# Five groups of context projections between the experts: one weight piece per block of products, two blocks per group at places of their own

## The chip, the cores and the metric

The kernel runs on one NeuronCore of a Trainium2 chip. It is one launch; everything is float32. The metric is the device time of one execution in microseconds; the median of three runs of the kernel before is 2745.36 us.

## The reference, cut to what matters

Two blocks of a model on a sequence of 256 tokens with 1024 features. The first block is a token mixer and then a feed-forward layer of 16 experts, each taking 34 of the 272 tokens. The second block is a bidirectional mixer of two branches (a gated delta rule, "gdn", and RWKV-7) that first runs over a context of 256 tokens to get its start states, and then over the tokens. The context's part does not depend on the first block, so the kernel computes it between the experts of the first block.

```python
# first block, per expert e (x16): xs are the 34 tokens that the router chose
hid = silu(xs @ w_gate[e]) * (xs @ w_up[e])      # w_gate, w_up: (1024, 2816)
y   = hid @ w_down[e] * g                        # w_down: (2816, 1024)
# second block, context: u_ctx is (256, 1024), w_in is (1024, columns)
a_ctx, b_ctx, _ = split(u_ctx @ w_in)
# gdn: k and v of the context: columns 512..1023 and 1024..1535, conv over time, silu, l2norm of k
# rwkv: k, v and the low-rank columns: 2064+512, 2064+1024 (512 each), 2064+1536 (256)
```

These five column groups are called k, v, rk, rv (512 columns each) and lo (256 columns). What is computed is the same before and after.

## The kernel before, in words

**The ring of weights.** All large weights pass through a ring of six slots in SBUF (`RING = 6`, a slot of `PIECE = 2816` floats in each of 128 partitions). `piece()` (in front of L170) numbers the pieces in the order in which the program will use them. SyncE (SP) issues them in that order at L871: piece n waits until the semaphore `piece_used` says that TensorE has released piece n-6. `piece_used` is one counter, so pieces are released in order too. An expert's gate and up weights come as 16 pieces (two for each 128 of the 1024 input features), its down weights as 8, each of 1408 KB with rows of 11 KB. `column_pieces(w, c0, cols)` makes two pieces of a column group of w_in, one for each half of the 1024 input features: for 512 columns 1024 KB each, with rows of 2 KB; for the 256 columns of lo 512 KB each, with rows of 1 KB.

**The experts' loop.** For each expert e (16) and each step k (8), TensorE runs `gate_up_pe(e, k)` (L3085): twelve products, in six pairs for six PSUM banks, matmuls at L3097, which need the two pieces of this step and release them at the last pair. After it come transposes of the hidden rows of expert e-1 (k = 0, 1; L3107), gathers of the chosen tokens for later experts (L2749, in expert 0 from k = 4 and in experts 1 and 2 in the middle of k = 1, 2), additions of finished experts (L3127) and the down products of expert e-1 (`down_pe`, L3120, k = 2 to 7). Expert e's hidden rows are made at its end: ScalarE's Silu of six banks (`silu_act`, L1119), VectorE's six products (L2048). The next expert's first matmul into a bank waits for that bank's product.

**Half steps.** The context's work is a Python generator on each of TensorE, ScalarE and VectorE. Each engine moves its generator on twice per step: in the middle of `gate_up_pe` (after the third of the six banks) and at the end of the step (not after k = 7). `slot_number(e, k)` is the number of the half step at the end of step (e, k); `until(n)` yields until half step n. The three engines count the same half steps, and all context work uses one PSUM bank, `bank_a`. What an engine does in one half step is queued in its program ahead of its share of the expert's next work, so a wait in a half step holds up the experts too.

**A column group before.** `AT_K = (0, 3)`, `AT_V = (2, 6)`, `AT_RK = (7, 1)`, `AT_RV = (8, 0)`, `AT_LO = (8, 4)`. Its two pieces stand in the ring's order behind the pieces of that step. TensorE's `project(name, cts)` (L2794) waits for both, computes two of four 128-column tiles (16 matmuls at L2802, listed as 32 by the profile), signals ScalarE, yields one half step, waits for ScalarE's copy out of `bank_a` (`landed_act`, L1136, copies at L1144), and computes the other two tiles; the first piece is released after 12 of those 16 matmuls, the second after 16. lo has two tiles only, so one block.

**What follows k.** VectorE convolves over time, one 128-row part per half step (L1800, L1802), ScalarE applies Silu (L1169), VectorE squares two parts (L1813), TensorE sums over features (L2854), ScalarE takes the root (L1175), VectorE the reciprocal and the product (L1815, L1816), and so for the other two parts one half step later. TensorE's first sum stands four half steps after the second block of products, in the middle of step (0, 6). Then TensorE turns k (L2814) at the ends of (1, 0) and (1, 1), and computes the gates at (1, 2). The group v goes through the conv and the Silu the same way, rk and rv through a time shift (L1911 to L1914) on VectorE.

## Time and profile before

| | |
|---|---|
| median of 3 runs | 2745.36 us (2738.47 to 2745.64) |
| the profiled execution | 2749.25 us, its span 2747.5 us |
| TensorE (PE) busy | 2425.6 us, 88% of the span |
| VectorE (DVE) busy | 893.0 us, 33% |
| ScalarE (ACT) busy | 447.5 us, 16% |
| GpSimd (POOL) busy | 85.5 us, 3% |
| moved by DMA | 789.10 MB, mean 287 GB/s |
| mean granted TensorE clock | 0.943 |

The profile's page gives busy times for each engine, the span in 40 equal slices of 68.7 us with the busy tenths of each engine in each slice, the DMA queues, the groups of instructions by source line with what ended their waits, and the DMA issues with their time to landing. A matmul's end is modelled, so a busy TensorE is not always TensorE at its peak. Busy shares are means over stages with different limits: the experts' loop lies in slices 6 to 26, the second block behind it. Answers to queries of the trace give the same for a stretch, an engine or a line.

### The profile page before, as it was taken

Reading aid. Unit: us, or ns where it says so; the run is one execution under the profiler, and the core shown is the slowest. Engines: PE = TensorE matmul, PEld = TensorE weight load, DVE = VectorE, ACT = ScalarE, POOL = GpSimd, SP = SyncE. Lnnn points to the kernel's source line nnn. Section 1 sums busy time; section 2 is a strip of 40 time slices with the busy share of each in tenths; the row PEclk is TensorE's granted clock in tenths of the full one; section 3 lists DMA queues with packets and bytes.
Section 4 is the critical chain, followed back from the end, with each engine's and each line's share of the span. In section 5 each row is a group of like instructions: output and inputs, shape, how many; then the busy total and the mean of one; then the engine's idle time right before and its main releaser. Section 6 shows DMA issues by size and latency. Waiting matters only on the chain. (4 is left out here: it accounts for less than half of the span.)

```text
span 2747.5 us, 42972 instructions
## 1 busy us (share of the span) xinstructions
PE 2425.6 (88%) x19453; PEld 1312.8 (48%) x19453; DVE 893.0 (33%) x1682; ACT 447.5 (16%) x810; POOL 85.5 (3%) x93
## 2 busy tenths in 40 slices
PE   7999799889999989999999999896595889599995
PEld 4544353333433434344444443275575877355552
DVE  3225534104222222313132221265556431332222
ACT  3112101101111101212121211231132220000001
POOL 0001000000000000000000000000001100000000
PEclk9998879999999999999999999998897999799998
DMA  5356348999999999999999999930010033479996
GB/s 191 116 180 225 143 173 324 400 418 377 411 422 423 408 378 380 421 412 403 415 408 421 413 400 408 393 109 16 2 39 2 4 128 123 167 290 422 422 423 279
DMA packets 129442, 789.10 MB, mean 287 GB/s; under 512 B 17493, under 2 KB 19805, under 8 KB 65133
## 3 DMA queue, kind: packets, MB, share of 16 engines
q1 hardware_dynamic: 125805, 773.78, 69.7%
q0 software_dynamic: 3456, 12.58, 1.2%
q8 instruction: 153, 2.51, 0.4%
q14 instruction: 28, 0.23, 0.0%
HBM read 774.79 MB, written 11.53 MB: 286 GB/s over the span
## 5 line engine op out<-in xcount | busy, mean ns | idle before, releaser
L3097 PE MATMUL bank<-ring,arena 128*34 128x462 f32 (+1 forms) x3072 | 680.3, 579 | 78.1 <-DMA ring<-in_w_up 57.5
L3097 PEld LDWEIGHTS bank<-ring,arena 128*34 128x34 f32 x3072 | 176.6, 114 | 444.4 <-issue 421.2
L3120 PE MATMUL bank<-ring,arena 128*34 128x512 f32 (+1 forms) x1536 | 339.4, 559 | 1.6 <-DMA ring<-in_w_down 1.0
L3120 PEld LDWEIGHTS bank<-ring,arena 128*34 128x34 f32 x1536 | 102.3, 112 | 220.7 <-issue 200.2
L311 PE MATMUL bank<-arena,ring 128*128 128x256 f32 (+1 forms) x688 | 158.1, 392 | 3.4 <-ACT arena L1050 1.4
L311 PEld LDWEIGHTS bank<-arena,ring 128*128 128x128 f32 x688 | 133.2, 194 | 28.6 <-issue 1.9
L2048 DVE TENSOR_TENSOR arena<-arena,bank 34x462 f32<-34x462 f32 (+1 forms) x96 | 95.5, 1084 | 155.1 <-ACT arena L1119 154.8
L3576 PE MATMUL bank<-ring,arena 128*64 128x256 f32 x992 | 111.4, 380 | 6.9 <-DMA ring<-in_moe_w_up 6.1
L1119 ACT ACTIVATE arena<-bank 34x462 f32<-34x462 f32 (+1 forms) x96 | 85.7, 1040 | 193.7 <-PE bank L3097 193.6
L3576 PEld LDWEIGHTS bank<-ring,arena 128*64 128x64 f32 x992 | 74.0, 137 | 48.2 <-issue 17.2
L2995 PEld LDWEIGHTS bank<-arena 64*64 64x64 f32 x2304 | 72.8, 135 | 47.6 <-issue 47.2
L3558 PE MATMUL bank<-arena 128*128 128x512 f32 (+1 forms) x160 | 82.3, 646 | 9.4 <-DVE arena L2538 5.8
L334 PE MATMUL bank<-ring,arena 128*128 128x512 f32 (+1 forms) x288 | 85.3, 501 | 0.2 <-ACT arena L1050 0.2
L3493 PE MATMUL bank<-arena,ring 128*128 128x256 f32 x384 | 83.1, 379 | 0.0
L2995 PE MATMUL bank<-arena 64*64 64x64 f32 x2304 | 82.7, 221 | 0.0
L2004 DVE TENSOR_TENSOR arena<-arena,bank 128x256 f32<-128x256 f32 x40 | 15.0, 417 | 200.5 <-PE bank L2995 200.5
L3493 PEld LDWEIGHTS bank<-arena,ring 128*128 128x128 f32 x384 | 72.9, 190 | 9.9
L1154 ACT ACTIVATE arena<-bank 128x512 f32<-128x512 f32 x42 | 25.1, 597 | 317.6 <-PE bank L2995 212.8
L3599 PE MATMUL bank<-ring,arena 128*64 128x512 f32 x264 | 63.8, 612 | 2.7 <-DMA ring<-in_moe_w_down 2.0
L971 POOL TENSOR_TENSOR arena<-arena 128x256 f32<-128x256 f32 (+1 forms) x16 | 26.7, 1670 | 1259.4 <-ACT arena L1243 1258.7
L2802 PE MATMUL bank<-arena,ring 128*128 128x256 f32 x288 | 64.2, 381 | 1.3 <-DMA ring<-in_w_in 1.3
L376 PE MATMUL bank<-ring,arena 128*128 128x512 f32 (+1 forms) x136 | 59.0, 634 | 3.9 <-DVE arena L2400 2.7
(655 smaller groups left out, 2804.0 us busy)
## 6 DMA issues: line engine op xcount, KB each, us to landing
ring<-in_w_gate SPq DMA_DIRECT2D x128, 1408.0 KB, 13.0
ring<-in_w_up SPq DMA_DIRECT2D x128, 1408.0 KB, 12.5
ring<-in_w_down SPq DMA_DIRECT2D x128, 1408.0 KB, 10.7
ring<-in_w_in SPq DMA_DIRECT2D x46, 1024.0 KB, 7.3
ring<-in_moe_w_down SPq DMA_DIRECT2D x33, 1024.0 KB, 16.5
ring<-in_moe_w_gate SPq DMA_DIRECT2D x31, 1024.0 KB, 15.5
ring<-in_moe_w_up SPq DMA_DIRECT2D x31, 1024.0 KB, 17.7
ring<-in_ada_w SPq DMA_DIRECT2D x24, 1024.0 KB, 7.2
```

What stands on the lines that cost most here:

```text
L311: last = mm(ps[base + ct][:, 0:n_toks], w[:, k, ct * P:(ct + 1) * P], x[:, half * kts + k, :], start=half + k == 0, stop=half == len(views ...
L334: last = mm(ps[base + t][rows, 0:cols.stop - cols.start], x[:, half * kts + k, off:off + r], w[:, k, cols], start=half + k == 0, stop=half ...
L1119: ACTV(hid_rows(c), in_rows(ps[c][0:CAP, 0:n]), ACT.Silu).then_inc(silu_done, up(silu_done))
L2048: TT(hid_rows(c), hid_rows(c), in_rows(ps[c][SLOT:SLOT + CAP, 0:n]), ALU.mult).then_inc(hid_done, up(hid_done))
L2802: last = mm(bank_a[:, ct % 2 * SEQ:(ct % 2 + 1) * SEQ], views[k // 4][0][:, k % 4, ct * P:(ct + 1) * P], u2x_ctx[:, k, :], start=k == 0, s ...
L2995: last = mm(dst[r, q, :], lhs[r, q, :], rhs[r, q, :], start=True, stop=True)
L3097: last = mm(ps[c][row:row + CAP, 0:n], xsT[:, e, k, :], w[:, at:at + n], start=k == 0, stop=k == KT - 1)
L3120: last = mm(ps[6][row:row + CAP, c:c + n], hidT[:, j, :], w[:, at - m * PIECE:at - m * PIECE + n], start=j == 0, stop=j == FT - 1)
L3493: last = mm(ps[base + ct // 2][:, ct % 2 * SEQ:(ct % 2 + 1) * SEQ], views[k // kts][0][:, k % kts, ct * P:(ct + 1) * P], x[:, k, :], start ...
L3558: last = mm(ps[gather_bank(g, k)][:, 0:group_cols(g)], xn2_by8[:, t, k, :], oh[g % 2][:, t, 0:group_cols(g)], start=t == 0, stop=t == 1)
L3576: last = mm(ps[4][CAP2 * which:CAP2 * (which + 1), m * DE:(m + 1) * DE], x, weights[which][:, k, :], start=k == 0, stop=k == KT - 1)
L3599: last = mm(ps[6 + half][CAP2 * m:CAP2 * (m + 1), :], hidT2[:, f, CAP2 * m:CAP2 * (m + 1)], w[:, f, half * BANK:(half + 1) * BANK], start= ...
```

## The change

`column_pieces` is called for 256 columns and all 1024 input features, so a piece holds all that two tiles need: 1024 KB, rows of 1 KB. A group of 512 columns has two such pieces, and each stands in the ring's order behind the step at whose end its products are computed:

| group | before: both pieces, first block, second block | after: first piece and block | after: second piece and block |
|---|---|---|---|
| k | (0, 3) end, (0, 3) end, (0, 4) middle | (0, 3) end | (0, 5) end |
| v | (2, 6) end, (2, 6) end, (2, 7) middle | (2, 3) end | (2, 6) end |
| rk | (7, 1) end, (7, 1) end, (7, 2) middle | (7, 1) end | (7, 3) end |
| rv | (8, 0) end, (8, 0) end, (8, 1) middle | (7, 6) end | (8, 0) end |
| lo | (8, 4) end, one block, two pieces | (8, 4) end, one piece | |

`project` waits for one piece, computes 16 matmuls and releases the piece at the last of them. Ahead of the second block TensorE waits for the group's own signal (`group_read` or `shift_ready`), which ScalarE now gives after each block; VectorE takes two of these signals, at the half step of the second block instead of the one after it. What follows a group is counted from the second block as before, so k's sums now stand in the middle and at the end of step (1, 0) and its turnings in the middle and at the end of (1, 1). The number of matmuls and the bytes are the same; there is one piece and one DMA fewer (lo).

```diff
-        AT_K, AT_V, AT_CHUNKS = (0, 3), (2, 6), slot_number(3, 2)
-        AT_RK, AT_RV, AT_LO, AT_STEPS = (7, 1), (8, 0), (8, 4), slot_number(8, 6, 0)
+        AT_K, AT_V, AT_CHUNKS = ((0, 3), (0, 5)), ((2, 3), (2, 6)), slot_number(3, 2)
+        AT_RK, AT_RV, AT_LO, AT_STEPS = ((7, 1), (7, 3)), ((7, 6), (8, 0)), ((8, 4),), slot_number(8, 6, 0)
...
-        CONTEXT_GROUPS = [("k", AT_K, 512, 512), ("v", AT_V, 1024, 512), ("rk", AT_RK, 2064 + 512, 512),
-                          ("rv", AT_RV, 2064 + 1024, 512), ("lo", AT_LO, 2064 + 1536, 256)]
+        CONTEXT_GROUPS = [("k", AT_K, 512), ("v", AT_V, 1024), ("rk", AT_RK, 2064 + 512),
+                          ("rv", AT_RV, 2064 + 1024), ("lo", AT_LO, 2064 + 1536)]
...
-                for name, place, c0, cols in CONTEXT_GROUPS:
-                    if place == (e, k):
-                        context_pieces[name] = column_pieces(A["w_in_2"], c0, cols)
+                for name, places, c0 in CONTEXT_GROUPS:
+                    for pair, place in enumerate(places):
+                        if place == (e, k):
+                            context_pieces[name, pair] = column_pieces(A["w_in_2"], c0 + 2 * P * pair, 2 * P, halves=1)[0]
...
-                def landed_act(dst, cts, views, signal):
-                    for pair in range(cts // 2):
-                        if views and pair == cts // 2 - 1:
-                            act.wait_ge(piece_used, after(views))
-                        else:
-                            act.wait_ge(context_filled_act, due(act, context_filled_act))
-                        for ct in (2 * pair, 2 * pair + 1):
-                            last = ACTV(dst[:, ct, :], bank_a[:, ct % 2 * SEQ:(ct % 2 + 1) * SEQ], ACT.Copy)
-                        if pair == cts // 2 - 1:
-                            last.then_inc(signal, up(signal))
-                        else:
-                            last.then_inc(context_read_act, up(context_read_act))
-                            yield from until(at[0] + 1)
+                def landed_act(dst, name, places, signal):
+                    for pair, place in enumerate(places):
+                        yield from until(slot_number(*place))
+                        act.wait_ge(piece_used, context_pieces[name, pair][3] + 1)
+                        for ct in range(2):
+                            last = ACTV(dst[:, 2 * pair + ct, :], bank_a[:, ct * SEQ:(ct + 1) * SEQ], ACT.Copy)
+                        last.then_inc(signal, up(signal))
...
-                for place, col, dst in ((AT_K, 4, kT_c), (AT_V, 8, vT_c)):
-                    yield from until(slot_number(*place) + 1)
-                    dve.wait_ge(group_read, due(dve, group_read))
+                for places, col, dst in ((AT_K, 4, kT_c), (AT_V, 8, vT_c)):
+                    yield from until(slot_number(*places[-1]))
+                    dve.wait_ge(group_read, due(dve, group_read, 2))
...
-                yield from until(slot_number(*AT_RK) + 1)
+                yield from until(slot_number(*AT_RK[-1]))
...
-                yield from until(slot_number(*AT_RV) + 1)
+                yield from until(slot_number(*AT_RV[-1]))
...
-                def project(name, cts):
-                    views = context_pieces[name]
-                    for _, slot, count, _ in views:
+                def project(name, places, signal):
+                    for pair, place in enumerate(places):
+                        yield from until(slot_number(*place))
+                        if pair:
+                            pe.wait_ge(signal, due(pe, signal))
+                        w, slot, count, _ = context_pieces[name, pair]
                         pe.wait_ge(slot, count)
-                    for pair in range(cts // 2):
-                        for ct in (2 * pair, 2 * pair + 1):
+                        for ct in range(2):
                             for k in range(KT):
-                                last = mm(bank_a[:, ct % 2 * SEQ:(ct % 2 + 1) * SEQ], views[k // 4][0][:, k % 4, ct * P:(ct + 1) * P],
-                                          u2x_ctx[:, k, :], start=k == 0, stop=k == KT - 1)
-                                if ct == cts - 1 and k % 4 == 3:
-                                    last.then_inc(piece_used, up(piece_used))
-                        if pair < cts // 2 - 1:
-                            token = for_act(last)
-                            yield from until(at[0] + 1)
-                            copied_by_act(token)
+                                last = mm(bank_a[:, ct * SEQ:(ct + 1) * SEQ], w[:, k, ct * P:(ct + 1) * P], u2x_ctx[:, k, :],
+                                          start=k == 0, stop=k == KT - 1)
+                        last.then_inc(piece_used, up(piece_used))
...
-                yield from until(slot_number(*AT_K))
+                yield from until(slot_number(*AT_K[0]))
                 pe.wait_ge(u2x_ready, due(pe, u2x_ready, 2))
-                yield from project("k", 4)
+                yield from project("k", AT_K, group_read)
```

## Rows read from the trace of the kernel before

**Rows 1.** The page, part 2: busy tenths of the DMA engines in 40 slices.

```profile
DMA  5356348999999999999999999930010033479996
```

**Rows 2.** Windows: stretch, length, busy us by engine, granted clock, DMA share, GB/s.

```profile
377.00:500.00 123.00, 116.89 (x536) 48.01 (x536) 38.50 (x62) 20.10 (x27) 0.00 (x0) 0.96 0.84 330
500.00:600.00 100.00, 84.25 (x382) 28.43 (x380) 8.58 (x10) 6.56 (x8) 0.00 (x0) 0.93 1.01 423
```

**Rows 3.** Waits of TensorE, 500 to 1750 us: total, times, longest.

```profile
PE bank L3097 <- DMA ring<-in_w_up: 57.5, 28, 4.1
```

**Rows 4.** Timeline of SP (start, duration): issues at 489, v, rk, rv.

```profile
488.90 0.33 SPq L871 DMA_DIRECT2D ring<-in_w_down  x1
...
607.23 0.33 SPq L871 DMA_DIRECT2D ring<-in_w_gate  x1
623.36 0.33 SPq L871 DMA_DIRECT2D ring<-in_w_up  x1
...
978.36 0.43 SPq L871 DMA_DIRECT2D ring<-in_w_gate  x1
994.66 0.33 SPq L871 DMA_DIRECT2D ring<-in_w_up  x1
...
1065.32 0.43 SPq L871 DMA_DIRECT2D ring<-in_w_up  x1
1081.64 0.33 SPq L871 DMA_DIRECT2D ring<-in_w_down  x1
```

**Rows 5.** DMA issues, us to landing: those of 607.23, 623.36, 978.36, 1065.32.

```profile
ring<-in_w_gate SPq DMA_DIRECT2D x1, 1408.0 KB, 14.4
...
ring<-in_w_up SPq DMA_DIRECT2D x1, 1408.0 KB, 5.8
...
ring<-in_w_gate SPq DMA_DIRECT2D x1, 1408.0 KB, 12.6
...
ring<-in_w_up SPq DMA_DIRECT2D x1, 1408.0 KB, 13.5
```

**Rows 6.** Windows around v's hole and over lo's products.

```profile
612.00:632.00 20.00, 20.00 (x94) 11.34 (x95) 6.04 (x9) 7.53 (x12) 0.00 (x0) 1.00 0.72 291
1115.00:1130.00 15.00, 14.77 (x71) 8.03 (x68) 2.81 (x6) 2.36 (x4) 0.00 (x0) 1.00 1.01 424
```

**Rows 7.** Windows in which lo's 1 KB and rk's 2 KB rows stream.

```profile
1110.60:1113.40 2.80, 2.14 (x13) 0.51 (x11) 0.00 (x0) 0.00 (x0) 0.00 (x0) 1.00 1.12 370
...
970.40:975.40 5.00, 3.90 (x20) 1.31 (x18) 0.55 (x1) 0.00 (x0) 0.00 (x0) 1.00 1.06 393
```

**Rows 8.** Timeline of TensorE: v's first block of products.

```profile
608.28 7.14 PE L2802 MATMUL bank<-arena,ring 128*128 128x256 f32 x32 [1.10 <-DMA ring<-in_w_in]
```

**Rows 9.** Timeline of TensorE, 430 to 451 us, with waits in brackets.

```profile
431.02 1.32 PE L2854 MATMUL bank<-arena,consts 128*128 128x512 f32 x2 [2.71 <-DVE arena L1813]
432.28 3.94 PE L3097 MATMUL bank<-ring,arena 128*34 128x462 f32 x12
...
440.28 1.13 PE L2854 MATMUL bank<-arena,consts 128*128 128x512 f32 x2 [1.44 <-DVE arena L1813]
441.33 4.92 PE L3097 MATMUL bank<-ring,arena 128*34 128x484 f32 x24
...
450.83 5.70 PE L3097 MATMUL bank<-ring,arena 128*34 128x484 f32 x24 [1.96 <-DVE arena L2048]
```

**Rows 10.** Groups of VectorE, 377 to 500 us: busy, mean ns, idle before.

```profile
L1815 DVE RECIPROCAL arena<-arena 128x512 f32<-128x512 f32 x2 | 6.7, 3352 | 5.5 <-ACT arena L1175 5.5
L2048 DVE TENSOR_TENSOR arena<-arena,bank 34x462 f32<-34x462 f32 (+1 forms) x6 | 5.9, 1057 | 0.0
...
L1813 DVE TENSOR_TENSOR arena<-arena 128x512 f32<-128x512 f32 x2 | 1.4, 686 | 1.3 <-ACT arena L1169 1.3
```

**Rows 11.** Timelines of ScalarE and VectorE: first root's table load; copy after turning.

```profile
432.43 1.28 ACT L1175 ACT_TABLE_LOAD   x1 [2.28 <-PE bank L2854]
...
457.37 0.55 DVE L2042 COPY arena<-bank 128x374 f32<-128x374 f32 x1 [1.86 <-PE bank L3107]
```

More of the change, by code:

```diff
@@ L1162, in context_act @@
                     act.wait_ge(norm_std_ready, own(act, norm_std_ready))
-                for place, name, dst, asked in ((AT_K, "k", kT_c, pad_ready), (AT_V, "v", vT_c, gdn_in_ready)):
-                    yield from until(slot_number(*place))
+                for places, name, dst, asked in ((AT_K, "k", kT_c, pad_ready), (AT_V, "v", vT_c, gdn_in_ready)):
+                    yield from until(slot_number(*places[0]))
                     act.wait_ge(asked, due(act, asked))
-                    yield from landed_act(pad_c[:, :, 2:2 + SEQ], 4, context_pieces[name], group_read)
+                    yield from landed_act(pad_c[:, :, 2:2 + SEQ], name, places, group_read)
                     yield from until(at[0] + 3)
@@ L1206, in context_act @@
                     yield from until(at[0] + 2)
-                yield from until(slot_number(*AT_RK))
+                yield from until(slot_number(*AT_RK[0]))
                 act.wait_ge(pads7, due(act, pads7))
-                yield from landed_act(sh_c[:, :, 1:1 + SEQ], 4, context_pieces["rk"], shift_ready)
+                yield from landed_act(sh_c[:, :, 1:1 + SEQ], "rk", AT_RK, shift_ready)
                 yield from until(at[0] + 2)
@@ L1804, in context_dve @@
                             yield from until(at[0] + 1)
-                    if place == AT_K:
+                    if places == AT_K:
                         dve.drain().then_inc(gdn_in_ready, up(gdn_in_ready))
                     dve.drain().then_inc(silu_asked, up(silu_asked))
-                    if place == AT_K:
+                    if places == AT_K:
                         two = lambda n: kT_c[:, 2 * n:2 * n + 2, :].rearrange("p h t -> p (h t)")
@@ L1909, in mixed @@
                     tmp = mix_c[:, 0:len(dsts), :]
-                    dve.wait_ge(shift_ready, due(dve, shift_ready))
+                    dve.wait_ge(shift_ready, due(dve, shift_ready, len(dsts) // 2))
                     in_order(TT(tmp, x[:, :, 0:SEQ], x[:, :, 2:2 + SEQ], ALU.add))
@@ L1942, in context_dve @@
                     yield from until(at[0] + 1)
-                yield from until(slot_number(*AT_LO))
+                yield from until(slot_number(*AT_LO[0]))
                 mixed([wlc, alc], 12).then_inc(lo_asked, up(lo_asked))
@@ L2874, in context_pe @@
                 last.then_inc(gates_ready, up(gates_ready))
-                yield from until(slot_number(*AT_V))
+                yield from until(slot_number(*AT_V[0]))
                 pe.wait_ge(act_asked, due(pe, act_asked, 2))
-                yield from project("v", 4)
+                yield from project("v", AT_V, group_read)
                 yield from until(AT_CHUNKS - 2)
@@ L2958, in context_pe @@
                         yield from until(at[0] + 1)
-                yield from until(slot_number(*AT_RK))
+                yield from until(slot_number(*AT_RK[0]))
                 read_by_dve(last_state[1])
-                yield from project("rk", 4)
+                yield from project("rk", AT_RK, shift_ready)
                 yield from until(at[0] + 2)
@@ L2969, in context_pe @@
                     yield from until(at[0] + 1)
-                yield from until(slot_number(*AT_RV))
+                yield from until(slot_number(*AT_RV[0]))
                 pe.wait_ge(root7, due(pe, root7))
-                yield from project("rv", 4)
+                yield from project("rv", AT_RV, shift_ready)
                 yield from until(at[0] + 2)
@@ L2981, in context_pe @@
                     read_by_dve(token)
-                yield from until(slot_number(*AT_LO))
-                yield from project("lo", 2)
+                yield from until(slot_number(*AT_LO[0]))
+                yield from project("lo", AT_LO, shift_ready)
                 yield from until(AT_STEPS)
```

8 lines of the change are left out of this document (4 added, 4 removed).

## The prediction

> **What bounds the kernel now.** I read the page first: in the slices of the experts (about slice 8 to 25) the DMA line is at nine tenths or more with two visible dents [rows 1]. Then the windows: from 377 to 500 us, which is expert 0 from its fourth step and the start of expert 1, the 16 DMA engines are busy 0.84 of the time and TensorE 116.9 of 123 us; from 500 us the DMA share is 1.01 at 423 GB/s with TensorE idle 16 of 100 us [rows 2]. So there are two regimes. Up to 488.9 us, the last issue that came after the queue had run dry for want of a release [rows 4], TensorE sets the pace and holes in the DMA stream cost nothing. After it the stream of weights sets the pace: between 500 and 1750 us TensorE's longest wait in total is for a landing, 57.5 us in 28 times [rows 3]. In that second regime a hole in the stream is lost for good, since every later piece lands later by it. A piece of an expert (1408 KB, 1.442 MB) takes 1.442/0.423 = 3.4 us of the stream.
>
> **Where the holes are.** SP issues piece n only after TensorE has released piece n-6. Before, both pieces of a context group are released only inside the second block of products: 7.1 us of products [rows 8], half a step, then most of another 7 us. The six slots run out. For v: the last issue ahead of the hole is at 607.23 and lands 14.4 later, at 621.6; the next issue is only at 623.36 and lands 5.8 later, at 629.2 [rows 4, 5]. That is 7.5 us between two landings where 3.4 are needed: a hole of 4.1. For rk: 978.36+12.6 = 991.0 and 994.66+5.8 = 1000.5, so 9.5-3.4 = 6.1. For rv: 1065.32+13.5 = 1078.8 and, with the same 5.8, 1081.64+5.8 = 1087.4, so 8.6-3.4 = 5.2 [rows 4, 5]. Together 15.4 us. The window around v's hole gives more, 20 x (1.01-0.72) = 5.8 [rows 6], because a window counts the ragged start and end too; at that ratio of 1.4 the three are worth 22 at most. lo, which has one block and not two, leaves no hole: the share is 1.01 in the window of its products [rows 6]. That is what the change makes of the others. k's hole lies in TensorE's regime.
>
> **The change, part by part.**
> (1) v, rk, rv: each block needs one piece and releases it at its end, three or more steps from its sister. A block then holds a slot for about 7 us while the other slots hold up to five pieces, 17 us of stream. The ring doesn't run dry as long as TensorE isn't late already; around these places it has the 16 us in 100 spare [rows 2]. Removed: 15.4 us, of which I take all, as at lo [rows 6]; bounds 10 (a third stays, as TensorE is near its limit around expert 7's start) and 22.
> (2) Weight rows of 1 KB in place of 2 KB. lo already has them: while its pieces stream, the rate is 370 GB/s at share 1.12, that is 330 per full share, against 393 at 1.06 = 371 while rk's stream [rows 7]. A piece of 1.049 MB costs 3.18 against 2.83 us, so 0.35 more; by the plain rates 2.83 against 2.67, 0.17 more. The middle, 0.26, for the six pieces of v, rk, rv: 1.6 us lost (1.0 to 2.1). k's two lie in TensorE's regime and cost nothing; if the stream were the bound there, 0.5. lo's piece is one issue in place of two: 0, its rows stay 1 KB.
> (3) v's conv on VectorE now has two of its four parts ahead of expert 2's products instead of one. Both lie beside the last step of TensorE's expert 2, and v's Silu moves one half step forward. 0, and the stream is the bound there; if that cover were gone, the nearest row is the wait for VectorE's products at expert 1's start, 2.0 [rows 9]. rv's mix moves ahead of the copy and addition of expert 8's second step: 0 for the same reason. No step is moved past a DMA issue on POOL or SP other than the pieces themselves.
> (4) k, the part that costs. Its second block moves three half steps later, and with it the chain conv, Silu, square, sum, root, reciprocal. Before, the first sum stands in step 6 of expert 0 and waits 2.7 us for its square (starts at 431.02), the second waits 1.4 (440.28); expert 1's first matmul waits 2.0 for VectorE's products (450.83) [rows 9]. Now the first sum falls into the middle of expert 1's first step, the second to its end, and the first turning of k behind the extra gather of its second step. TensorE is the bound here, and everything of every step is queued behind these waits.
> - Expert 1's start: the same wait of 2.0. ScalarE's Silu of k comes ahead of expert 0's six, but ends before the gather that VectorE's products wait for: 0 more.
> - First sum: VectorE's six products take 5.9 us [rows 10], then the square 0.7: 6.6. TensorE starts some 1.2 us after they do (the first takes 1.06 [rows 10], then its signal), and has half a step (half of the 5.70 in rows 9, 2.85) to do: it waits 6.6-4.05 = 2.6, against 2.7 before. 0.
> - Second sum: before, ScalarE's table load began 1.4 us after the first sum did (432.43 [rows 11]); it took 1.28, root and product about 0.7 each like the square, the reciprocal 3.35 [rows 10]: 7.4. Now the copy of the turned hidden rows (0.55 [rows 11]) and the square follow: 8.7, or 7.4 if the table load comes ahead of the wait. TensorE has the sum (1.1), half a step (2.5) and the turning (450.83+5.70 to 457.37, 0.8) [rows 9, 11]: 4.4. It waits 3.0 to 4.3 against 1.4: 1.6 to 2.9 more; I take 1.8, as no other work of ScalarE stands between its six Silus and the root.
> - First turning: TensorE waits for VectorE's scaling of the gathered rows, about as long as the square (0.69 [rows 10]), and a drain: 1.0 where nothing waited.
> - Clock: the stretch has a granted clock of 0.96 [rows 2], so TensorE was at 1.2 instead of 2.4 GHz for a few us of it. After the 2.7 us wait the half step at 432.28 took 3.94 where half of the full step at 441.33 is 2.46 [rows 9], 1.5 lost. The later waits are longer; some of the dip falls into a wait. 0 to 3 more, I take 0.7.
> Sum: 2.6 to 6.9 us; value 1.8+1.0+0.7 = 3.5, near the low end, since the rows give each link and only the clock is open. Bounds 1 and 8.
>
> **The sum.** -15.4 +1.6 +3.5 = -10.3 us. The profiled execution took 2749.25 us, 1.75 more than its span of 2747.5; less 10.3 it would take 2739.0. It is 3.9 above the median of the three runs, 2745.4, so on their scale I predict 2735.1 us.
>
> **One rule weighed.** The Trainium skill, page "DMA: Bandwidth & Descriptors", section Specifications, gives 512 B as the least transfer for line rate. By it part (2) would be 0. The trace differs, with 330, 371 and 423 GB/s for rows of 1, 2 and 11 KB (an expert's pieces) [rows 2, 7], and the sum goes by the trace.
>
> **Rivals.**
> A. As forecast, a gain of 8.3 to 14 us: 2731 to 2737. Chance 0.55.
> B. The holes close in part, or k's chain costs more (one more table load and two clock dips: 3.5+1.3+3 = 7.8): gain 2 to 8, at 15.4-1.6-7.8 = 6.0 near 2739. For it: TensorE's wait for landings is small around experts 3 to 7, so time given back there may meet TensorE's own limit. Against: it still waits for landings after v's block. Chance 0.27.
> C. The change doesn't do what it says: the single block still empties the ring, since TensorE is late at (7,1) and (7,6) anyway, and holes of some 5 us stand at six places in place of three. About 2745. Against: 7 us of products against 17 us of queued stream. Chance 0.06.
> D. Slower: the k chain at expert 1. Its waits and the small turning products leave TensorE at 1.2 GHz through most of the stretch from 446 to 489 us. At half clock 43 us of work cost some 21 more; with k's own 3.5 and part (2), -15.4+1.6+3.5+21 = +10.7, 2756 us. It decides from the point where the low clock costs more than 10.3 us, half of that stretch. For it: the dip in rows 9; against: it lasted only for about a half step there, though the wait ahead of it was as long. Chance 0.07.
> E. Rows of 1 KB cost what rows of 2 KB cost in the queue, as their shares overlap with other packets in the windows [rows 7]: part (2) is 0 and the gain 11.9, 2733.5. This is what the page's rule above would give. Chance 0.05.
>
> **How the numbers follow.** What a measurement can tell from no change is about 0.3%, 8.2 us. Faster by more: A and E, 0.60. Within: B and C, 0.33. Slower by more: D, 0.07. The range takes in A, B and E: from the wide end of the holes (22-1.0-3.5 = 17.5, 2728, less a little spread of the runs, 2727) to B's poor end (gain 2, 2743, with spread 2744).
>
> **What would show it.** Right: in the profile after, the issues after v, rk and rv follow one another without the 16 us wait on the projection's line, the DMA share in windows around (2,6), (7,1), (8,0) is 1.0, and the stretch from the k group to SP's first issue bound by landings (488.9 before) is 3 to 4 us longer, with waits of 2.6 and 3 to 4 us ahead of the two sums. Wrong: new idle on SP behind a single block; a granted clock at the lower level for long in 446 to 489; TensorE's waits for landings vanishing around expert 3 or 7, which would say that TensorE is the bound there.

## The result, and the profile after

The kernel after takes 2726.43 us (median of 4 runs, 2720.79 to 2730.77) beside 2743.68 us for the kernel before on the same chip (4 runs, 2738.47 to 2745.64): a ratio of 0.9939, 95% interval 0.9914 to 0.9964, or 17.2 us less. Two later comparisons gave 13.6 and 14.7 us less (below). I had forecast 10.3 less, 2735.1 us, and 2727.0 as the low end of the range. The sign was right, the size was too small, and none of the rivals had a gain of 17.

The profiled execution took 2720.79 us (span 2719.0), 28.5 less than the profiled one of before. 11.4 of these arise before the end of step (0, 3), where the change has nothing: that step ends 384.8 us after the start, and 396.2 in before. So stretches of after stand 11.4 earlier than those of before up to here, and I compare them from that point on.

The page's DMA line, for [rows 1], and below it the GB/s of the same 40 slices:

```profile
DMA  5356367999999999999999999830000033479996
GB/s 193 113 187 227 144 227 307 409 418 424 412 424 423 409 401 414 411 421 405 413 405 421 417 396 408 337 117 1 10 30 2 3 135 118 169 312 422 422 422 277
```

The same line of before:

```profile
GB/s 191 116 180 225 143 173 324 400 418 377 411 422 423 408 378 380 421 412 403 415 408 421 413 400 408 393 109 16 2 39 2 4 128 123 167 290 422 422 423 279
```

The two dents of which I spoke are not in the tenths, which are 9 in both kernels there: I had misplaced them. They are in the GB/s of before, 377 in slice 10 and 378 and 380 in slices 15 and 16. After has 424, 401 and 414.

The windows that answer to [rows 2] (stretch, length, busy us of PE, PEld, DVE, ACT, POOL with counts, granted clock, DMA share, GB/s):

```profile
365.60:488.60 123.00, 116.23 (x538) 47.72 (x538) 39.20 (x64) 18.78 (x26) 0.00 (x0) 0.96 0.84 330
488.60:588.60 100.00, 88.31 (x410) 34.60 (x408) 8.54 (x10) 7.21 (x10) 0.00 (x0) 0.96 1.01 422
```

The two regimes are as before: TensorE is busy 116 of 123 us in the first, the stream of weights is full in the second. TensorE's waits in the second, 488.6 to 1732 us (what waited, for what, total us, times, longest), for [rows 3]:

```profile
PE bank L3089 <- DMA ring<-in_w_up: 42.1, 27, 4.1
...
PE bank L3089 <- DVE arena L2043: 5.1, 2, 2.6
PE bank L2960 <- DVE arena L1922: 3.1, 1, 3.1
```

TensorE waits 15.4 us less for landings (57.5 before) and 5.7 more for VectorE's work: it has come nearer to its own limit. SP's waits for the release by the projection, first in before (500 to 1750 us), then in after (488.6 to 1732):

```profile
SPq L871 <- PE bank L2802: 58.3, 8, 15.9
```

```profile
SPq L872 <- PE bank L2799: 48.0, 7, 7.1
```

The longest falls from 15.9 to 7.1 us. And the timeline of SP over v's two blocks in after (start, duration of the issue, line, what), for [rows 4]. The `in_w_in` is v's second piece, whose block runs from 597.46 to 604.6:

```profile
581.33 0.44 SPq L872 DMA_DIRECT2D ring<-in_w_in  x1
583.55 3.69 SPq L872 DMA_DIRECT2D ring<-in_w_gate  x1
592.81 0.33 SPq L872 DMA_DIRECT2D ring<-in_w_up  x1
...
595.38 0.33 SPq L872 DMA_DIRECT2D ring<-in_w_gate  x1
597.58 0.33 SPq L872 DMA_DIRECT2D ring<-in_w_up  x1
604.67 0.33 SPq L872 DMA_DIRECT2D ring<-in_w_gate  x1
```

The pause over the block is 7.1 us (597.58 to 604.67), where before had 16.1 over two of them (607.23 to 623.36). The piece issued at 597.58 lands 15.2 us later, so 7 us without an issue empties nothing.

**A finer scale.** Executions of one kernel differ by up to 22 us (below), of which the first 390 us alone have 12 in these traces. Inside the experts they repeat to about 1 us, at a few steps to 2 or 3. So I take from each trace when TensorE releases the up piece of a step (the end of the step's gate and up products), count from the release of (0, 3), and subtract the first execution of before. This table stands under everything below. "start" is (0, 3) itself from the beginning of the span, "tail" the time behind (15, 7).

```
us       before  before  after  after  after  k as    k as     pieces    v chain  blocks    k one   rows of
                 again          again  2      before  before 2 of 256,   late     one step  step    8 KB
                                                               old places         apart     apart
(0,7)      50.1   +0.0   -8.5   -8.5   -8.5   +0.0    +0.0     +0.0      -8.5     -8.5      +2.8    -8.5
(1,3)      92.7   +0.1   -0.1   -0.0   -0.1   -2.3    -2.3     -2.3      -0.0     -0.1      +2.9    -0.1
(2,3)     170.8   +0.1   +0.2   -0.1   -0.2   -2.5    -2.4     -2.4      +2.0     +1.9      +4.9    -0.1
(2,7)     231.4   -0.6   -6.6   -8.3   -6.5   -9.4    -9.3     -2.1      -5.4     -4.2      -2.4    -9.1
(4,5)     373.9   +1.0   -8.2   -8.5   -8.3  -10.6   -10.6     -2.5      -7.1     -7.0      -4.1    -9.5
(7,0)     573.8   +1.2   -6.9   -6.2   -6.6  -10.5   -10.1     -2.3      -6.9     -6.2      -2.7    -9.5
(9,5)     816.4   +0.6  -17.0  -16.9  -17.1  -18.9   -20.1     -2.7     -16.9    -13.5     -13.4   -16.4
(15,7)   1349.3   -0.2  -17.8  -17.1  -18.1  -21.2   -21.3     -6.3     -20.6    -14.6     -14.6   -18.2
start     396.2   -0.8  -11.4   -4.1  -11.9   -0.2    -2.7     -4.6      -4.3     -1.0      -0.3   -11.9
tail     1002.0   -2.8   +0.8   +0.1   -0.1   +0.0    -2.1     -0.5      +0.8     -3.1      -3.0    -2.1
```

The three executions of after give the parts of the sum: k costs nothing at (1, 3), v gains 8.0 to 8.5 from there to (4, 5), rk and rv 8.4 to 8.9 from (4, 5) to (9, 5). Together 17.1 to 18.1 us at (15, 7), and the forecast said 3.5 lost, 3.6 and 10.3 gained. (Against the second execution of before, v has 9.0 to 9.4 and rk and rv 8.0 to 8.5.)

Where v's share ends is my choice, and it matters by 1 to 2 us. At (7, 0), still ahead of rk, the three executions of after are only 6.2 to 6.9 us ahead. Between (6, 4) and (7, 1) each of them has 3.4 us of low clock, and both executions of before have none; in the first of after the products of (7, 0) take 6.62 us in place of 4.92. Counted up to (7, 0), v gains 6.2 to 6.7 and rk and rv 10.2 to 10.7. Whether that low clock is a result of v's gain or a matter of its own was not tried.

### The profile page after: what moved, and what is told of

Read it like the earlier page. It is cut to its first block and busy times, and to the rows that moved or that the text cites. A ratio compares the mean times of both kernels' runs of the same rounds, so it can differ in the third digit from the quotient of the medians.

```text
span 2719.0 us, 42973 instructions
## 1 busy us (share of the span) xinstructions
PE 2408.9 (89%) x19453; PEld 1310.2 (48%) x19453; DVE 893.3 (33%) x1682; ACT 446.1 (16%) x809; POOL 85.6 (3%) x93
## 5 line engine op out<-in xcount | busy, mean ns | idle before, releaser
L3089 PE MATMUL bank<-ring,arena 128*34 128x462 f32 (+1 forms) x3072 | 672.3, 574 | 67.3 <-DMA ring<-in_w_up 42.1
L311 PEld LDWEIGHTS bank<-arena,ring 128*128 128x128 f32 x688 | 133.4, 195 | 28.5 <-issue 1.9
## 6 DMA issues: line engine op xcount, KB each, us to landing
ring<-in_w_down SPq DMA_DIRECT2D x128, 1408.0 KB, 10.7
```

The costliest lines, as they stand in the source:

```text
L311: last = mm(ps[base + ct][:, 0:n_toks], w[:, k, ct * P:(ct + 1) * P], x[:, half * kts + k, :], start=half + k == 0, stop=half == len(views ...
L3089: last = mm(ps[c][row:row + CAP, 0:n], xsT[:, e, k, :], w[:, at:at + n], start=k == 0, stop=k == KT - 1)
```

## The experiments

The edits shown are shortened to their sense. In the kernels that were run, a table of half steps per group stands in place of the lines with places.

**Both kernels again.** No edit.

> The kernel before, unchanged, for a second profile of it. The comparison of the two profiles at hand, aligned at the end of expert 0's step 3, says: k costs nothing (0.0 us at step (2,0)), v gives 8.4 us, rk and rv together 9.3. Theory V1 (v's hole is worth 8 us, as the stream loses more than the gap between two landings): step (4,5) ends 373.9 us after step (0,3) here too, within 1 us. Theory V2 (v is worth about 4 us as forecast, and some 4 us of the first profile are chance): this stretch is some 370 us here. The time up to step (0,3), which differed by 11 us between the two profiles though nothing of the change lies in it, should differ again by several us.

> The changed kernel, unchanged, for a second profile and more rounds. If the first result stands: ratio to before 0.994. From the end of step (0,3), step (2,0) at 145.8 us, (4,5) at 365.7, (9,5) at 799.4, (15,7) at 1331.5, each within 1.5 us if chance is small inside this stretch. If chance explains the gain beyond the forecast, (15,7) comes near 1338.

Measured: before 2739.87 (17 runs, 2727.85 to 2746.81); after 2726.23 (6 runs, 2716.66 to 2728.66), ratio 0.9946 (0.9926 to 0.9966). The table's columns agree to about 1 us at most steps (1.7 at (2, 7) of after), and the start differs by 7 us between the two executions of after. What follows: differences of several us inside the experts are those of the kernels, and the 11.4 of the 28.5 us between the first two profiles that arise ahead of (0, 3) are not.

**k as before.** The kernel after, with k's group alone in its old form (two pieces of 512 columns, blocks half a step apart):

```diff
-AT_K = ((0, 3), (0, 5))   # two pieces of 256 columns, two blocks
+AT_K = (0, 3)             # column_pieces(w, c0, 512), blocks at (0, 3) end and (0, 4) middle
```

> The changed kernel with k as before: two pieces of half the features with rows of 2 KB, both at (0,3), second block half a step later, chain of k as before; v, rk, rv, lo as changed. Theory K0 (k's new waits are made good by other waits and clock dips that fall away): from step (0,3) to (2,0) the same 145.7 us as both, total as the changed kernel, ratio to before 0.994. Theory K1 (my forecast: k's chain costs 3.5 us): (2,0) the same or 3 us earlier than in the changed kernel and the total 3 us below it, 0.993.

Measured: 2722.58 us (6 runs), ratio 0.9931 (0.9904 to 0.9958). At (1, 3) it is 2.3 us ahead of after. But up to there its instructions are those of before, but for a drain on ScalarE after k's first copy, and it is 2.3 us ahead of before too. The steps (0, 4) to (0, 7) take the same time in both to 0.01 us. Then the granted clock parts them. First before, then this kernel: the window over gates and step (1, 3), and TensorE's timeline in it (start, duration, line):

```profile
479.60:486.40 6.80, 6.80 (x25) 3.11 (x26) 0.71 (x4) 3.42 (x7) 0.00 (x0) 0.50 0.97 414
...
476.98 4.69 PE L2866 MATMUL bank<-arena 128*128 128x16 f32 x32
481.61 7.27 PE L3097 MATMUL bank<-ring,arena 128*34 128x484 f32 x24
```

```profile
479.40:486.20 6.80, 6.80 (x44) 3.48 (x45) 0.72 (x4) 3.42 (x7) 0.00 (x0) 1.00 1.01 421
...
477.79 3.75 PE L2883 MATMUL bank<-arena 128*128 128x16 f32 x32
481.46 4.92 PE L3114 MATMUL bank<-ring,arena 128*34 128x484 f32 x24
```

Before runs these 6.8 us at a granted clock of 0.50, 1.2 GHz: 0.9 + 2.4 = 3.3 us lost. The kernel with k as before has its low clock at 451.9 to 455.4 instead, where it costs 1.0 (step (1, 0) takes 11.27 against 10.28). Net 2.3.

**The same, once more, beside after.**

> The kernel with k as before and v, rk, rv as after, once more, beside the kernel after on the same chip. Theory (k is decided by where TensorE's low clock falls, and the first such run was 2.3 us ahead of the kernel after at (1,3) and 3 to 4 ahead at (15,7)): 2 to 4 us ahead of the kernel after at (1,3) again, with 6.8 us of low clock between (0,3) and (1,3) against 10.2, and a median 2 to 4 us below the other's. Rival (the first comparison was the luck of one profile): the two differ by less than 1 us at (1,3).

> The kernel after, once more. Theory: (1,3) within 0.2 us of the kernel before's and (15,7) 17 to 18 us ahead of it, counted from the end of (0,3); the median near 2726.

Measured: again 2.3 us ahead at (1, 3), 6.8 us of low clock against 10.2, and 3.2 ahead of after at (15, 7), as the theory had it. Its medians were not: 2727.75 (7 runs) against 2725.55 for after (11 runs, ratio to before 0.9955, 0.9940 to 0.9969), 2.2 above and not below. The spread of the first 390 us can hide 3 us. So after is not shown to be beaten by the mixed kernel.

All the times of low clock between the releases of (0, 3) and (1, 3), as begin (length), counted from (0, 3):

```
before                      35.577 (3.4)                83.364 (6.8)     (1,3) at 92.7
before again                36.188 (3.4)                83.975 (6.8)              92.8
k as before                 35.437 (3.4)  55.917 (3.4)                            90.4
k as before 2               35.545 (3.4)  56.025 (3.4)                            90.4
pieces of 256, old places   35.564 (3.4)  56.044 (3.4)                            90.4
after (3 executions)        52.5-52.7 (3.4)  59.3-59.5 (3.4)  86.6-86.8 (3.4)     92.6
k one step apart            45.6 (6.8)                  86.6 (6.8)                95.6
```

On TensorE the first five run the same work at the same times up to 50 us. Those whose first low stretch begins at 35.56 or earlier have the next at 56, those in which it begins at 35.58 or later at 83. That goes together in five of five; that the one causes the other was not tried. Nor do five executions tell whether the kernel decides it or the single execution: both late ones are of before, but nothing that sets before apart from the other two kernels moved TensorE ahead of 50 us.

**Pieces of 256 columns at the old places.** The new pieces and the release after each block, but both pieces of a group behind the same step, blocks half a step apart (and rv at (8, 0) again):

```diff
-AT_K, AT_V   = ((0, 3), (0, 5)), ((2, 3), (2, 6))
-AT_RK, AT_RV = ((7, 1), (7, 3)), ((7, 6), (8, 0))
+AT_K, AT_V   = ((0, 3), (0, 3)), ((2, 6), (2, 6))
+AT_RK, AT_RV = ((7, 1), (7, 1)), ((8, 0), (8, 0))
```

> Pieces of 256 columns and all features (rows of 1 KB) as changed, but both pieces of a group stand at the old place and the second block comes half a step after the first, as before. So the first piece is released after its own block, 7 us earlier than before, and the second block is where it was. Theory F (the form, that is the early release, closes the holes): nearly the whole gain, (15,7) near 1334 us after (0,3). Theory P (the places matter: 14 us of TensorE's products within 17 us keep the following pieces' slots busy): holes shrink by about the time of one piece, 3.4 us each, from 4, 6, 5 to 1, 3, 2, less 0.5 each for the rows: gain 8, (15,7) near 1341.

Measured: 2736.18 us (10 runs), ratio 0.9994 (0.9975 to 1.0012). From (1, 3) to (4, 5) it gains 0.2 us, from (4, 5) to (9, 5) 0.2, so (15, 7) comes at 1343.0, later than either theory had it. Behind (9, 5) it wins 3.6 more, for which I have no cause; the kernel with v's chain late wins 3.7 there too. Its TensorE over v's blocks (in brackets the wait and who ended it), SP there, and the window:

```profile
597.24 7.14 PE L2821 MATMUL bank<-arena,ring 128*128 128x256 f32 x32 [0.24 <-DMA ring<-in_w_in]
606.98 4.00 PE L3111 MATMUL bank<-ring,arena 128*34 128x484 f32 x12 [2.59 <-DMA ring<-in_w_up]
610.91 7.42 PE L2821 MATMUL bank<-arena,ring 128*128 128x256 f32 x32
...
604.41 0.33 SPq L876 DMA_DIRECT2D ring<-in_w_up  x1
618.35 0.33 SPq L876 DMA_DIRECT2D ring<-in_w_gate  x1
...
605.50:625.50 20.00, 18.52 (x80) 9.24 (x80) 6.27 (x9) 7.06 (x10) 0.00 (x0) 0.91 0.80 324
```

The first block starts as soon as its own piece has landed, but then TensorE waits 2.59 us for the next expert pieces, and its half step runs at the low clock (4.00 us). The two blocks still follow each other with half a step between, SP still has a pause of 13.9 us, and the stream falls to 324 GB/s. So neither the form of the pieces nor the early release brings the gain. It comes with the places: the blocks, and each block's piece in the ring's order, a step or more apart. Whether places apart would do it with the old pieces was not run.

**v's chain one half step later.** The kernel after, with v's conv and Silu put back to where before had them:

```diff
-yield from until(slot_number(*places[-1]))                      # conv of k, v on VectorE
+yield from until(slot_number(*places[-1]) + (places == AT_V))
...
-yield from until(at[0] + 3)                                      # Silu on ScalarE
+yield from until(at[0] + (4 if name == "v" else 3))
```

> The changed kernel, but v's conv on VectorE and its Silu on ScalarE come half a step later, as before; the pieces and the blocks of products stay at (2,3) and (2,6). Both profiles of the kernel before show a second, small hole in the weight stream at expert 3's steps 2 to 4 (about 652 to 672 us: 387 and 359 GB/s against 425), and TensorE waits 1.2 us for v's Silu in expert 3's step 1. Both profiles of the changed kernel show neither. Theory S (the chain's half step: TensorE is late at expert 3 because it waits for the Silu, and that empties the ring a second time): the wait is back, expert 3's steps 2 to 4 stream at under 415 GB/s, and step (4,5) ends 367 to 369 us after step (0,3) in place of 365.5. Theory H (the second hole is an echo of the first: TensorE was late by the products): no second hole, (4,5) at 365.5.

Measured: 2725.16 us (1 run; before 2742.07 beside it). TensorE's wait for v's Silu is back, as in before. First this kernel, then before:

```profile
636.18 0.63 PE L2828 MATMUL bank<-consts,arena 128*128 128x128 f32 x4 [1.19 <-ACT arena L1173]
636.74 2.59 PE L3111 MATMUL bank<-ring,arena 128*34 128x484 f32 x12
```

```profile
645.47 0.63 PE L2814 MATMUL bank<-consts,arena 128*128 128x128 f32 x4 [1.17 <-ACT arena L1169]
646.02 4.26 PE L3097 MATMUL bank<-ring,arena 128*34 128x484 f32 x12
```

Step (3, 2) takes 9.08 us, 7.86 in after. The second hole of before (387 GB/s at 652 to 672 us) does not come back with it; the stream of this kernel there:

```profile
643.00:663.00 20.00, 20.00 (x108) 7.67 (x106) 5.88 (x13) 2.73 (x5) 0.00 (x0) 1.00 1.01 425
```

From (1, 3) to (4, 5) it gains 7.1 us, 0.9 to 1.4 less than after, which neither theory had as it stands. But nothing points to the Silu: this kernel is 1.2 to 1.5 us behind after at (3, 1) already, ahead of the wait, 2.4 to 2.7 at (3, 2), and 1.2 to 1.4 again at (3, 5). It also has low clock in step (2, 1), which takes 11.48 us where before and after take 9.58. So has the kernel with k one step apart (11.63), whose v is that of after, and it gains 7.0. The wait of 1.2 costs nothing that can be told, as the stream runs on beneath it. In before the same wait is followed by a half step at the low clock, and step (3, 2) takes 10.73; behind it the stream has a second hole (next section).

**Blocks one step apart.** v at (2, 5) and (2, 6), rk at (7, 1) and (7, 2), instead of three and two steps:

```diff
-AT_V, AT_RK = ((2, 3), (2, 6)), ((7, 1), (7, 3))
+AT_V, AT_RK = ((2, 5), (2, 6)), ((7, 1), (7, 2))
```

> The changed kernel with v's first block at (2,5) instead of (2,3) and rk's second at (7,2) instead of (7,3), so that both groups' blocks are one step apart; the rest as changed. My forecast's account (a hole appears where products outlast the queued pieces): 14.2 us of products and 10 of the step between them against some 20 us of queued stream, so the ring nearly runs dry: holes of 0 to 3 us each, (4,5) at 365.5 to 368.5, (7,5)-(7,2) as changed or 1 to 3 later. Rival (any two places apart are enough): as the changed kernel within 1 us, (4,5) at 365.5, (7,7) at 651.

Measured: 2730.55 us (1 run). From (1, 3) to (4, 5) it gains 6.9 us, like the two kernels with the same low clock in step (2, 1) (7.1 and 7.0; 11.67 us here) whose v is three steps apart. Its stream is full over v's blocks and behind them (426, 424 and 424 GB/s in the three windows from 606 to 666 us). From (4, 5) to (9, 5) it gains 6.5 instead of 8.4 to 8.9. One whole step between the blocks is enough at v. At rk the one execution leaves it open: the kernel with rows of 8 KB, whose blocks are those of after, gains only 6.9 in this stretch.

**k one step apart.** k at (0, 3) and (0, 4), the sums back at the end of step (0, 6) and in the middle of (0, 7):

```diff
-AT_K = ((0, 3), (0, 5))
+AT_K = ((0, 3), (0, 4))
```

> The changed kernel with k's second block at (0,4) instead of (0,5), so that k's two sums fall into the end of step (0,6) and the middle of (0,7), and k is turned at the end of (1,0) as before. Theory K0 (k's place is worth nothing since TensorE's waits add up to the same): step (2,0) at 145.6 to 145.9 us after (0,3) as in both kernels. Theory K1 (the chain across the experts' boundary costs, and clock dips hide it): (2,0) at 143 as in the kernel with k as before, where one low-clock stretch fewer was seen, total 2 to 3 us below the changed kernel.

Measured: 2729.8 us (4 runs), ratio 0.9936 (0.9911 to 0.9962). It is 2.9 us behind before and after at (1, 3): neither theory had that. It has 13.6 us of low clock (table above), and its second sum waits longer than in any other kernel here. The window and the sum:

```profile
441.60:448.50 6.90, 6.38 (x14) 1.45 (x14) 3.98 (x3) 4.24 (x5) 0.00 (x0) 0.51 0.00 2
...
442.12 2.08 PE L2868 MATMUL bank<-arena,consts 128*128 128x512 f32 x2 [4.44 <-DVE arena L1817]
```

Low clock of 6.8, 10.2 and 13.6 us goes with (1, 3) at 90.4, 92.6 and 95.6. The waits ahead of the two sums and of expert 1's first products are 1.46 + 4.44 + 2.03 = 7.9 us here and 6.1 in before: 1.8 more. So the places of k's chain act here through the clock and through the waits they move, about equally when compared with before.

**Rows of 8 KB.** The context's pieces of 1024 KB are read from contiguous rows of another matrix, all else as after. So this kernel leaves out the context's own weights, and where the rows lie changes together with their length:

```diff
+rows = A["w_down"][e].rearrange("(p j) c -> p (j c)", j=FT)   # 128 rows, 8 KB of each
+pieces[-1] = (rows[:, 0:2048], ring slot, ...)
```

> The changed kernel with its nine context pieces read from a contiguous part of other weights, in rows of 8 KB in place of 1 KB, same bytes; so the context's values are other ones (that part of the computation is changed). It measures what short rows cost. From the trace of before: 330 GB/s at 1 KB, 421 at 11 KB, so 0.7 us a piece by full shares, and 0.4 by the time between landings (2.86 against 2.46). v, rk, rv and lo are 7 pieces in the stretch that the stream bounds: (15,7) 2.8 to 4.9 us earlier than in the changed kernel. If short rows cost nothing: 0.

Measured: 2717.04 us (1 run; its start is one of the early ones). v's second piece lands 2.48 us behind the piece ahead of it; in after 2.86 (592.98 to 595.84), and in before, with its 2 KB rows, v's first 2.64 (602.90 to 605.54). But at (15, 7) it is 18.2 ahead of before, where after is 17.1 to 18.1. Seven pieces at 0.4 us would be 2.7, the low end of what I had expected; 0 to 1 of it arrives. 1.0 is there behind v and is lost again around experts 7 and 8, where the stream has a hole in this kernel (after, at 1008.5 to 1028.5 us, moves 371 GB/s and not 350):

```profile
1008.00:1028.00 20.00, 20.00 (x93) 9.07 (x90) 3.05 (x2) 0.00 (x0) 0.00 (x0) 0.94 0.86 350
```

TensorE is busy for all 20 us of it, so I read it thus: what the stream wins, TensorE does not take up.

## Why the prediction was right or wrong

**The two regimes and the cause of the gain: right.** The stream sets the pace behind 489 us, the holes came from two blocks half a step apart, and they go when the blocks stand apart. The old places with the new pieces gain nothing. Rivals C and D did not happen; D's stretch, 446 to 489 us in before, has 10.2 us of low clock in after, not 43. (D's price was too low besides: where 6.8 us of low clock cost 3.3 us here, a stretch low for 43 us would lose 21, but 43 us of full-speed work at half the clock would take 43 more.)

**Part (1), v: the mechanism was right, the size wrong, and this is the step that failed.** I took v's hole as the excess of one difference of landings, 4.1 us, and let the window's 5.8 widen the range only. The window was nearer. Windows of before around v's hole stand in [rows 6]; these are those behind it, and over rk's and rv's holes:

```profile
652.00:672.00 20.00, 20.00 (x108) 7.68 (x106) 5.72 (x14) 2.73 (x5) 0.00 (x0) 1.00 0.98 387
984.00:1004.00 20.00, 20.00 (x92) 10.76 (x91) 6.65 (x12) 2.60 (x5) 0.00 (x0) 1.00 0.68 273
1072.00:1092.00 20.00, 20.00 (x99) 10.64 (x100) 6.79 (x11) 1.32 (x4) 0.00 (x0) 1.00 0.70 282
```

And after, over the stretch of v and behind it, then of rk and rv:

```profile
602.00:622.00 20.00, 18.09 (x96) 7.28 (x94) 15.42 (x27) 7.29 (x11) 0.00 (x0) 1.00 1.01 423
622.00:642.00 20.00, 20.00 (x107) 7.79 (x107) 5.41 (x11) 2.75 (x4) 0.00 (x0) 1.00 1.01 425
642.00:662.00 20.00, 18.48 (x97) 6.92 (x95) 5.25 (x11) 0.73 (x2) 0.00 (x0) 1.00 1.01 425
...
971.70:991.70 20.00, 20.00 (x96) 9.90 (x94) 1.52 (x2) 1.94 (x3) 0.00 (x0) 1.00 0.99 398
...
1051.70:1071.70 20.00, 20.00 (x105) 6.63 (x106) 8.46 (x15) 0.66 (x2) 0.00 (x0) 1.00 1.00 410
```

Before moved 291 GB/s around v's hole where 425 is full: 20 x (1 - 291/425) = 6.3 us. The landing behind the issue at 623.36 is not the only late one: of the landings up to 676 us, where 3.4 us apart is full rate, one pair is 7.5 us apart and others 4.6, 4.0 and 4.25, some 6.8 us in excess together. One difference does not see them. At 652 to 672 before has a second hole, 20 x (1 - 387/425) = 1.8 us (3.1 in the second execution, at 359 GB/s), which I had not looked for. 6.3 + 1.8 to 3.1 less 0.5 for the rows is 7.6 to 8.9; measured 8.0 to 8.5. (The page alone gives nearly this: 68.7 x (424 - 377)/424 = 7.6 for slice 10.) The second hole follows the step with the Silu wait and the low clock. The kernel with pieces of 256 columns at the old places has all three too (375 GB/s at 645.5 to 665.5 us). The kernel with v's chain late has the wait and neither the low clock nor the hole (425 GB/s), so the wait alone doesn't make it. Whether the low clock does or the ring still shallow from the first hole stays open. The low clock is a rival for part of v's gain as well: from (1, 3) to (4, 5) the two executions of before have 17.1 and 23.9 us of it, the three of after 6.8 to 10.2. No run separates it from the holes.

**rk and rv: right, with what was forecast or a little less.** 11.3 - 1.0 = 10.3 forecast, 8.4 to 8.9 measured from (4, 5) on, 10.2 to 10.7 from (7, 0) on. (rv's hole by landings is 5.4, not 5.2: the piece issued at 1081.64 took 6.0 us to land, and I had used v's 5.8.) Here the bytes say more than the landings too (273 and 282 GB/s: 7.2 and 6.7 us), but not all comes back: after runs at 398 to 412 GB/s here where v has 425. That is my reason for the lower bound of part (1) (TensorE is near its limit around expert 7's start), in a size of 20 x (2 - 398/425 - 410/425) = 2 us in these two windows; the six windows from 951.7 to 1071.7 us (424, 398, 404, 391, 412 and 410 GB/s) together lack 5.2 us, their rows of 1 KB included. The waits for VectorE's work (5.7 us more) and the experiment with 8 KB rows say the same. So v gave 4.4 to 4.9 us more than forecast and rk and rv 1.4 to 1.9 less; with the border at (7, 0), v gave 2.6 to 3.1 more and rk and rv 0.1 less to 0.4 more.

**Part (2), 1 KB rows: right per piece, not seen in the total.** Landing behind landing, a piece takes 2.86 us against 2.64, 0.22 more, where I had 0.26. The rule of 512 B that I weighed (the Trainium skill, page "DMA: Bandwidth & Descriptors", section Specifications) does not hold for the single piece: 2.86, 2.64 and 2.48 us with rows of 1, 2 and 8 KB. The total comes out as the page has it, though, and as I read the traces for another reason: the kernel with 8 KB rows wins 0 to 1 us over after, and TensorE is near its bound where most of the pieces stand. Rival E's result of 0 for this part is about right, its mechanism is not.

**Part (3), v's chain half a step earlier: 0, right.** The wait that it removes is made up within three steps while the stream is the bound, in the one execution that puts it back.

**Part (4), k: each wait but one as forecast, the clock not; the term of 3.5 us came out at 0.** TensorE in after, from the start of expert 1, for [rows 9]:

```profile
430.93 2.82 PE L3089 MATMUL bank<-ring,arena 128*34 128x484 f32 x12 [1.96 <-DVE arena L2043]
436.28 1.12 PE L2846 MATMUL bank<-arena,consts 128*128 128x512 f32 x2 [2.53 <-DVE arena L1808]
437.33 4.14 PE L3089 MATMUL bank<-ring,arena 128*34 128x462 f32 x12
...
443.58 1.65 PE L2846 MATMUL bank<-arena,consts 128*128 128x512 f32 x2 [1.30 <-DVE arena L1808]
...
452.47 0.63 PE L2806 MATMUL bank<-consts,arena 128*128 128x128 f32 x4 [0.98 <-DVEq L1813]
```

And on ScalarE and VectorE, for [rows 10, 11]:

```profile
433.37 1.28 ACT L1170 ACT_TABLE_LOAD   x1
437.44 0.69 ACT L1170 ACTIVATE arena<-bank,small 128x512 f32<-128x512 f32 x1 [2.79 <-PE bank L2846]
...
438.17 3.35 DVE L1810 RECIPROCAL arena<-arena 128x512 f32<-128x512 f32 x1 [2.03 <-ACT arena L1170]
```

The waits are 1.96 (forecast 2.0), 2.53 (2.6), 1.30 (3.0 to 4.3) and 0.98 (1.0). The table load does come ahead of the wait, the shorter of my two cases, and from sum to sum it is 443.58 - 436.28 = 7.3 us (forecast 7.4). The second wait is short because the half step in it took 4.14 us instead of 2.5: it ran at the low clock. I counted the low clock as a cost on top of the waits; here 1.6 us of the one stand in place of the other. With that, waits come to 6.8 us against 2.71 + 1.44 + 1.96 = 6.1 in before, 0.7 more.

The rest is the baseline. Over (0, 3) to (1, 3) after and before both have 10.2 us of low clock, and k comes out at 0, within 0.1 us; what makes up the 0.7 us of waits was not looked for. Against the kernels that run k as before with 6.8 us of low clock, k's move costs 2.3 us at (1, 3). That is 0.7 of waits and 3.4 us more of low clock at half speed, 1.7; the forecast had 1.8 + 1.0 of waits and 0.7 of clock. So the second sum's 1.8 is the link that failed, and the clock was worth more than I gave it. At (9, 5) pairs on the same chip are 2.1 and 3.0 us apart. At (15, 7) they are 3.2 and 4.1 apart, but that cannot be charged to k: the kernel with v's chain late has k as in after and is 20.6 ahead there, against 21.2 and 21.3. The two executions of before that were traced were both of the costlier kind, and I took the low clock of before for a fixed part of it. The trace of before has a window at 0.50 over 479.6 to 486.4, inside the stretch that I had costed; I had not looked at what it cost, 3.3 us.

In sum: forecast +3.5 (k), -3.6 (v), -10.3 (rk, rv), together -10.3 but for rounding; measured 0, -8.0 to -8.5, -8.4 to -8.9, and -0.2 to -0.9 behind (9, 5), together -17.1 to -18.1 at (15, 7). Two terms were mis-sized: v's hole, by 2.6 to 4.9 us as the border is drawn, and k's chain, by 3.5 (1.2 against k as before).

## What to carry to other kernels

Size a hole in a stream by the bytes that are missing from windows over it and over the two windows behind it, not by the one widest gap between landings. A consumer that needs several pieces in a row should be cut so that at least one whole step of other work stands between its parts; smaller pieces and earlier releases alone gained 0.4 us of 17. Before costing a chain on a busy TensorE, look up where its low clock already falls: 3.4 us more or less of it was worth 1.7 us here, more than the 0.7 of waits that moved, and a comparison of single steps, aligned at a common event, shows it where totals don't.

## What the runs showed of the hardware that I had not expected

The low clock repeats, and yet turns on very little. In all six traced executions with k at its new places (1, 3) came 92.6 to 92.7 us after (0, 3), with low clock at the same three times to 0.3 us. But of five executions whose work on TensorE is the same to 0.05 us for 50 us, three had it at 56 us and two at 83, at 2.3 us between them. What it costs depends on where it falls: 6.8 us at (1, 3) cost 3.3, and 3.4 us at (1, 0) cost 1.0.

It also goes with a shift of the first block, which is the same code in all kernels here. Step (0, 3) ends at 384.8, 392.1 and 384.3 us in the three executions of after. First the window of 150 to 200 us and ScalarE's longest sum of waits up to 384 us in the first of them, then in the second:

```profile
150.00:200.00 50.00, 46.72 (x271) 21.61 (x270) 5.45 (x20) 10.18 (x23) 0.00 (x0) 1.00 0.55 187
...
ACT arena L1089 <- PE bank L2685: 59.5, 6, 15.6
```

```profile
150.00:200.00 50.00, 46.72 (x212) 21.37 (x212) 5.05 (x18) 9.00 (x21) 0.00 (x0) 0.83 0.40 137
...
ACT arena L1089 <- PE bank L2685: 66.7, 6, 22.8
```

A granted clock of 0.83 in place of 1.00 goes with 7.2 us more of waiting for TensorE, nearly all of the 7.3 between the two. This alone is two fifths of the effect that was to be measured. Runs of one kernel spread over up to 22 us (2723.61 to 2745.51 in one of the experiments); how much of that is the first block was traced only in the profiled executions, 384.3 to 396.2 us.
